# A gated delta rule kernel: triangular inverses from 16x16 blocks on all 128 partitions instead of 32x32 blocks on 64

## What is computed

```python
kb = k * beta[..., None]
a_mat = jnp.where(strict, jnp.einsum('bhncd,bhnsd->bhncs', kb, k) * decay, 0.0)
l_mat = a_mat + eye
t_mat = lax.linalg.triangular_solve(l_mat, jnp.broadcast_to(eye, l_mat.shape), left_side=True,
                                    lower=True, unit_diagonal=True)
u = jnp.einsum('bhncs,bhnsd->bhncd', t_mat, v * beta[..., None])
...
def step(state, inp):
    qd, qkc, uc, wc, kd, gl = inp
    v_new = uc - jnp.einsum('bhcd,bhde->bhce', wc, state)
    o = jnp.einsum('bhcd,bhde->bhce', qd, state) + jnp.einsum('bhcs,bhse->bhce', qkc, v_new)
    state = state * gl[..., None, None] + jnp.einsum('bhcd,bhce->bhde', kd, v_new)
    return state, o
```

## Time and profile before

| | |
|---|---|
| median of 3 runs | 2483.99 us (2482.22 to 2491.87) |
| profiled execution, its time | 2487.21 us |
| profiled execution, its span | 2485.4 us |
| PE busy in the span | 2140.9 us (86%) |
| DVE busy in the span | 1197.3 us (48%) |
| ACT busy in the span | 850.7 us (34%) |
| mean granted PE clock | 0.933 of 2.4 GHz |

### The profile page before, as it was taken

The page is one execution under the profiler, slowest core; times in us unless marked ns, Lnnn a source line. Parts: engine busy times, 40 slices in busy tenths (PEclk is TensorE's granted clock), DMA queues, the critical chain, the costliest instruction groups (busy, mean ns, idle before and its releaser), DMA issues. The chain is left out here.

```text
span 2485.4 us, 29399 instructions
## 1 busy us (share of the span) xinstructions
PE 2140.9 (86%) x11304; PEld 1677.7 (67%) x11304; DVE 1197.3 (48%) x2121; ACT 850.7 (34%) x1348; POOL 492.6 (20%) x280
## 2 busy tenths in 40 slices
PE   3589999999999999567984789999899886999978
PEld 2467878787787878545763577666676655788767
DVE  5658677585958577345223433324223232522243
ACT  2365253435345352134112132433433442510121
POOL 0220202021110202034354221111111101432240
PEclk7789999999999999778997899999999998999989
DMA  6123232222323231164112211120211105211222
GB/s 272 36 73 99 61 101 90 69 88 69 94 63 104 65 101 48 41 236 147 45 35 80 76 56 34 51 77 26 79 50 34 60 26 195 85 51 43 76 85 85
DMA packets 126523, 199.22 MB, mean 80 GB/s; under 512 B 56324, under 2 KB 87812, under 8 KB 125232
## 3 DMA queue, kind: packets, MB, share of 16 engines
q1 hardware_dynamic: 126384, 197.34, 24.6%
HBM read 155.17 MB, written 42.11 MB: 79 GB/s over the span
## 5 line engine op out<-in xcount | busy, mean ns | idle before, releaser
L709 PE MATMUL p_job<-h_hi,w_hi 128*128 128x512 f32 x784 | 332.0, 424 | 45.9 <-DVE w_lo L850 23.1
L711 PE MATMUL p_job<-h_hi,w_lo 128*128 128x512 f32 x784 | 312.6, 399 | 0.0
L710 PE MATMUL p_job<-h_lo,w_hi 128*128 128x512 f32 x784 | 312.4, 398 | 0.0
L1691 PE MATMUL m_job<-h_hi,m_hi 128*128 128x512 f32 x592 | 262.0, 442 | 36.8 <-POOL m_lo L1527 36.8
L1693 PE MATMUL m_job<-h_hi,m_lo 128*128 128x512 f32 x592 | 238.4, 403 | 0.0
L1692 PE MATMUL m_job<-h_lo,m_hi 128*128 128x512 f32 x592 | 237.7, 402 | 0.0
L709 PEld LDWEIGHTS p_job<-h_hi,w_hi 128*128 128x128 f32 x784 | 151.6, 193 | 88.7 <-DVE w_lo L850 23.4
L1527 POOL TENSOR_TENSOR m_lo<-m_raw,m_hi 128x1024 fp32r<-128x1024 f32 x37 | 89.9, 2429 | 465.4 <-DVE m_hi L1799 465.4
L710 PEld LDWEIGHTS p_job<-h_lo,w_hi 128*128 128x128 f32 x784 | 151.7, 194 | 37.5 <-issue 8.2
L711 PEld LDWEIGHTS p_job<-h_hi,w_lo 128*128 128x128 f32 x784 | 151.2, 193 | 33.0
L1691 PEld LDWEIGHTS m_job<-h_hi,m_hi 128*128 128x128 f32 x592 | 115.3, 195 | 83.0 <-POOL m_lo L1527 37.5
(11 more groups left out here) (350 smaller groups left out, 4592.4 us busy)
## 6 DMA issues: line engine op xcount, KB each, us to landing
w_raw<-in_w SPq DMA_DIRECT2D x49, 512.0 KB, 3.6
m_raw<-in_w SPq DMA_DIRECT2D x37, 512.0 KB, 3.6
rows<-grows SPq DMA_DIRECT2D x32, 512.0 KB, 6.5
ada<-in_ada_w SPq DMA_DIRECT2D x8, 1536.0 KB, 12.5
e_raw<-in_w SPq DMA_DIRECT2D x24, 512.0 KB, 3.6
z_scr<-pre SPq DMA_DIRECT2D x16, 512.0 KB
o_scr<-oT SPq DMA_DIRECT2D x64, 128.0 KB, 1.8
ob<-o_scr SPq DMA_DIRECT2D x16, 512.0 KB, 4.2
```

What stands on the lines that cost most here:

```text
L709: nc.tensor.matmul(p_job[h][:], hi, h_hi[:, k, cut], start=(k == 0), stop=False)
L710: nc.tensor.matmul(p_job[h][:], hi, h_lo[:, k, cut], start=False, stop=False)
L711: last = nc.tensor.matmul(p_job[h][:], lo, h_hi[:, k, cut], start=False, stop=(k == KD - 1))
L1691: nc.tensor.matmul(p_job[h][:], hi, h_hi[:, k, cut], start=(k == 0), stop=False)
```

## The change

Blocks of 16x16 (`SUB`) take the place of 32x32 ones in the substitution. There are two of them in each 32x32 block, 128 in all, one to each partition: partitions 0 to 63 hold the upper left halves, 64 to 127 the lower right ones. The substitution has 15 steps instead of 31, in three `lane` entries of five steps, on (j+1)x(15-j) elements. Two new merges on PE (now `merge` 0 and 1, the old four are 2 to 5) make the 32x32 inverses from the 16x16 ones:

```diff
-LANE_STEPS = 8
+SUB = 16
+LANE_STEPS = 3
+MERGES = 6
+MERGE_ACT = (0, 0, 4, 5, 7, 8)
+MERGE_DVE = (0, 1, 4, 5, 6, 7)
@@ plan
-            behind.append((15, ("silu", j)))
+            behind.append((10, ("silu", j)))
...
     for q in range(LANE_STEPS):
         out.append(("lane", q))
-        send(5)
-        if ahead and q == 2:
-            out.append(("bcast", i))
-    out.extend([("lanes_out",), ("diag_in",)])
-    send(80 - sent)
+        send(2)
+    out.append(("lanes_out",))
+    send(10)
+    if ahead:
+        out.append(("bcast", i))
+    out.append(("diag_in",))
+    send(72 - sent)
     if ahead:
         out.append(("decay", i, 0))
-    for q in range(4):
+    for q in range(MERGES):
         out.append(("merge", q))
         send(4)
@@ stage_deltanet, tiles
-        nsq = PM[:].rearrange("p u t -> p (u t)")[:, 0:HALF]
-        nrm = PM[:].rearrange("p u t -> p (u t)")[:, HALF:2 * HALF]
+        nsq = sb("nsq", [P, HALF])[:]
+        nrm = sb("nrm", [P, HALF])[:]
@@ SP
-                            sp.dma_start(AL[0:LANES], io["a_lanes"]).then_inc(al_in, 16)
+                            for q in range(2):
+                                sp.dma_start(AL[lane_rows(q)], halves(io["a_lanes"], q)).then_inc(al_in, 16)
...
-                            sp.dma_start(io["u_lanes"], UL[0:LANES]).then_inc(ul_out, 16)
+                            for q in range(2):
+                                sp.dma_start(halves(io["u_lanes"], q), UL[lane_rows(q)]).then_inc(ul_out, 16)
                             sp.wait_ge(turned, g + 1)
-                            sp.dma_start(io["t_lanes"], TL[0:LANES]).then_inc(ul_out, 16)
+                            for q in range(2):
+                                sp.dma_start(halves(io["t_lanes"], q), TL[lane_rows(q)]).then_inc(ul_out, 16)
@@ ACT, merge
+                            if q == 1:
+                                for n in range(NB):
+                                    nc.scalar.activation(Uu[blk(n), :, n * BLK + SUB:(n + 1) * BLK],
+                                                         grid(p_turn, n * BLK, (n + 1) * BLK, SUB, 0, 16), ACT.Copy
+                                                         ).then_inc(merge_act, 1)
@@ PE, merge
                                 for u in range(2 * NT):
+                                    for n in range(NB):
+                                        left = TD[blk(n), u, corner(n).start:corner(n).start + SUB]
+                                        last = nc.tensor.matmul(p_mone[blk(n), u * SUB:(u + 1) * SUB],
+                                                                atu[blk(n), u, blk(n)], left, start=True, stop=True)
+                            elif q == 1:
+                                pe.wait_ge(vb_done, 4 * (g + 1))
+                                for u in range(2 * NT):
+                                    for n in range(NB):
+                                        last = nc.tensor.matmul(
+                                            p_turn[blk(n), u * SUB:(u + 1) * SUB], PF[blk(n), u, :],
+                                            Uu[blk(n), u, n * BLK + SUB:(n + 1) * BLK], start=True, stop=True)
+                                for u in range(2 * NT):
+                                    for n in range(NB - 1):
+                                        last = nc.tensor.matmul(
+                                            p_mtwo[blk(n), u * SUB:(u + 1) * SUB], Uu[blk(n), u, blk(n)],
+                                            PF[blk(n), u, 0:SUB], start=True, stop=True)
@@ DVE, lane and merge
-                            for j in range(4 * q, min(4 * q + 4, BLK - 1)):
-                                m, r, w = N_LANE * g + 2 * j, j + 1, BLK - 1 - j
+                            for j in range(5 * q, 5 * q + 5):
+                                m, r, w = N_LANE * g + 2 * j, j + 1, SUB - 1 - j
...
+                                nc.vector.scalar_tensor_tensor(PF[:, :, 0:SUB], grid(p_mone, 0, P, SUB, 0, 16),
+                                                               fold[:, 2 * SUB:2 * SUB + 1],
+                                                               bc(fold[:, 0:SUB], 1, 2 * NT), ALU.mult, ALU.add
+                                                               ).then_inc(merge_dve, 1)
+                            elif q == 1:
+                                for n in range(NB - 1):
+                                    at_col = corner(n).start
+                                    nc.vector.tensor_copy(TD[blk(n), :, at_col:at_col + SUB],
+                                                          grid(p_mtwo, n * BLK, (n + 1) * BLK, SUB, 0, 16)
+                                                          ).then_inc(merge_dve, 1)
```

More of the change, by code:

```diff
@@ L432, in blk, with halves, lane_rows, corner @@
             return slice(n * BLK, (n + 1) * BLK)
+        def halves(scratch, q):
+            return scratch[:, q * SUB:(q + 1) * SUB, q * SUB:(q + 1) * SUB]
+        def lane_rows(q):
+            return slice(q * LANES, (q + 1) * LANES)
+        def corner(n):
+            return blk(1) if n == 1 else blk(0)
         def grid(bank, lo, hi, w, n0, n1):
@@ L447, in _ @@
                 for dst, src in ((tri[:], io["tri"]), (conv_w[:], io["conv_w"]),
-                                 (adt[32:48, :], io["adt"])):
+                                 (adt[32:48, :], io["adt"]), (fold[:], io["fold"])):
                     sp.dma_start(dst, src).then_inc(cst, 16)
+                sp.wait_ge(u_zero, 1)
+                for lanes in (io["u_lanes"], io["t_lanes"]):
+                    sp.dma_start(lanes.rearrange("u s t -> u (s t)"),
+                                 U[0:LANES].rearrange("p c a t -> p (c a t)")[:, 0:BLK * BLK]).then_inc(lanes_zero, 16)
                 load(1)
@@ L500, in _ @@
                                 sp.wait_ge(u_zero, 2)
-                            sp.wait_ge(ul_out, 32 * (g + 1))
-                            for n in range(NB - 1):
-                                cut = blk(1) if n == 1 else blk(0)
-                                sp.dma_start(TD[blk(n), :, cut], io["t_lanes"][n * 2 * NT:(n + 1) * 2 * NT].rearrange(
+                            sp.wait_ge(ul_out, 64 * (g + 1))
+                            for n in range(NB):
+                                sp.dma_start(TD[blk(n), :, corner(n)], io["t_lanes"][n * 2 * NT:(n + 1) * 2 * NT].rearrange(
                                     "u t s -> t u s")).then_inc(diag_in, 16)
@@ L626, in _ @@
                                 act.wait_ge(nss_done, m)
-                            if i >= 2 and w == 0 and h == 0:
-                                act.wait_ge(merge_ready, 4 * g)
                             nc.scalar.activation(nsq, src, ACT.Square).then_inc(nsq_done, 1)
@@ L674, in _ @@
                                                      ACT.Copy, scale=-1.0).then_inc(merge_act, 1)
-                            elif q == 2:
+                            elif q == 4:
                                 nc.scalar.activation(PM[64:128, 0:8, :], grid(p_mone, 64, 128, 2 * BLK, 0, 8),
                                                      ACT.Copy).then_inc(merge_act, 1)
-                            else:
+                            elif q == 5:
                                 nc.scalar.activation(Uu[0:64, 0:8, 64:128], grid(p_turn, 0, 64, 2 * BLK, 0, 8),
@@ L786, in _ @@
                                 for u in range(2 * NT):
+                                    for n in range(NB):
[5 more added lines that the diff above has]
+                                for u in range(2 * NT):
+                                    for n in range(NB):
+                                        last = nc.tensor.matmul(
[6 more added lines that the diff above has]
+                                            PF[blk(n), u, 0:SUB], start=True, stop=True)
+                            elif q == 2:
+                                for u in range(2 * NT):
                                     for r, bank in enumerate((p_mone, p_mtwo)):
@@ L987, in _ @@
                             if q == 0:
-                                dve.wait_ge(nmul, 4 * min(i + 1, QK_HEADS))
+                                if g >= 1:
+                                    dve.wait_ge(merge_dve, N_DVE * g)
+                                else:
+                                    dve.wait_ge(fold_set, 1)
+                                nc.vector.scalar_tensor_tensor(PF[:, :, 0:SUB], grid(p_mone, 0, P, SUB, 0, 16),
[8 more added lines that the diff above has]
+                                                          ).then_inc(merge_dve, 1)
+                            elif q == 2:
```

80 lines of the change are left out of this document (42 added, 38 removed).

## The result

The changed kernel takes 2500.57 us in the median (2497.46 to 2505.11), the kernel before 2484.68 us in the runs beside it (2482.22 to 2491.87). The ratio is 1.0061, with a 95% interval from 1.0034 to 1.0088. So it is slower by 0.6%, where 2461 us and a range from 2443 to 2492 us had been forecast.

What follows compares the result with a forecast made beforehand. PE was taken as the bound, busy 107 of 113 us per iteration. Terms -42.0 + 28.0 - 2.5 - 6.3 = -22.8 us gave 2464.4 from 2487.2, so 2461 us in the median; range 2443 to 2492, its own 2448 to 2472.

Steps and rivals of the forecast that it cites:

- New matmuls: New merges 0 and 1 on PE: 352 records cost 4.0 us per iteration, +28.0 us over seven iterations.
- PE's waits, -42.0: PE in iterations 1 to 7: evacuation and square waits go, 30.6 us, plus 11.4 us of lower clock.
- The square wait: PE waiting for ACT's squares, 1.60 us at 349.82, 12.1 us in iterations 1 to 7; read as the same ACT backlog.
- The four sub-arrays do not take turns: Rival at new merges: no overlap into one bank, 11.5 us per iteration, 2526 us; chance 0.16, in full 0.09.
- Half as many moving columns: Part of the bigger-gain rival (chance 0.13, about 2447 us): narrow matmuls in the new merges at half price, -12 us.
- The wait at the first sum: Rival: substitution in one run makes ACT's square late, PE waits 2 us or more per iteration; 2489 us, chance 0.17.
- Iteration 0, -2.5: Iteration 0: silus moved forward on ACT take 2.5 of the 5.4 us that PE waits for a square.
- Iteration 8, -6.3: Iteration 8: merging starts 14.7 us earlier, two more merges with copies in the open cost 8.4; net -6.3 us.
- Copies, DMAs, start: 0: New ACT and DVE copies under cover of slices, lane transfers, and constants at stage start: no cost, start bound +1.
- iteration of 110.4 us: Length of one iteration that the profile after the change was to show.

Runs made afterwards that it cites:

- the kernel with 11 matmuls left: Changed kernel with 11 small matmuls standing for the new merges' 176 from iteration 2 on, output not the reference's; 2448.29 us.
- the one with the halves apart by four and placed later: Changed kernel with four slices between merge 1's two halves, first merge at slice 70, decay step behind it, two slices between the last two merges; 2473.45 us.
- the swapped: Changed kernel with merge 1's two halves in the other order, the p_mtwo matmuls ahead of the p_turn ones; 2498.17 us.
- the extended kernel: Kernel before the change, with 112 extra small matmuls at the head of its merge 1, results used nowhere; 2545.48 us.

## Why the prediction was wrong

**The step that failed** is "New matmuls", +28.0 us. It priced 352 records by the time of the sub-arrays and the change-over, and asked nothing about how they reach PE. As work the price was right: merge 0 held PE for 1.3 us as forecast, and with the stalls gone an iteration is 110.5 us, 3.3 over the 107.2 of the kernel with 11 matmuls left, where I had 4.0 for all of them. What was missing is the stall, 15.9 - 1.8 = 14.1 us in iterations 1 to 7, and the lower clock behind it. The changed kernel and the one with the halves apart by four and placed later differ by 114.4 - 110.5 = 3.9 us per iteration, 27 us in seven: 2.0 us of stall, the rest slow slices. That is almost the whole miss of +13.5 against -14. The rows of the kernel before could have raised the question: its merge 1 has 96 records at 10.4 ns, but only 192 instructions in a row, less than a block of 256. The density was there, the length was not.

The Trainium skill (Runtime: NRT & Kernel Launch, "Instruction fetch mechanics") says that each engine's sequencer refills its instruction memory in 16 KiB blocks of 256 instructions, and that the cost of crossing a block is mostly hidden. The packets here have that size. That the cost is hidden holds for the slices and for the old merges; it does not hold for 448 or 640 instructions in a row that PE would do in 2 to 3 us, where it is 1.6 to 2.3 us for the 448 and 3.4 us an iteration for the 640.

**PE's waits, -42.0.** Right in size: 5.5 us per iteration measured with the small matmuls nearly left out, 6.0 forecast. Half of the reason was wrong. The square wait was not the substitution's backlog "further on", but ACT's order; I had given that part of the change no value in iterations 1 to 7, so that the size came out is in part luck.

**The rivals.** The four sub-arrays do not take turns: 128 records into one bank in 1.26 us, against 4 us in turns. Half as many moving columns did not halve the price either: one sub-array's 32 records took 1.2 us with 32 columns and take 1.26 us with 16. The rule of the Trainium skill (TensorEngine Tiling (Array Packing), "Gotcha 1: PSUM Pressure") that different row tiles cannot use one bank at once does not show in these runs, where each row group writes partitions of its own. The wait at the first sum did not come either, although the substitution with its copy ended at 314.1 and not at 309.7: it took 7.6 us for my 7.2, and began 4 us late (306.5), behind a split that DVE ended only then. The 2489 us of that rival was right for an iteration that loses some 4 of its 6 us, not one that keeps them, as the text has it. I had a rival that lost by a slow merge, with the wrong mechanism.

**Iteration 0, -2.5.** Measured +0.3 (175.1 against 174.8 us): the silu went, the decay exponential and two table loads stand ahead of the square.

**Iteration 8, -6.3.** Measured -2.0. Merging starts 13.2 us earlier after the reset (1011.71 - 985.22 = 26.5 against 39.7 us), where I had 14.7. The merges take 26.4 us from the first to the chunk loop:

```profile
1011.71 1.90 PE L819 MATMUL p_mone<-TD,at 32*32 32x16 f32 x128 [5.39 <-issue]
...
1015.30 1.72 PE L825 MATMUL p_turn<-U,PF 32*32 32x16 f32 x114 [0.64 <-issue]
...
1019.04 1.68 PE L830 MATMUL p_mtwo<-PF,U 32*32 32x16 f32 x83 [1.80 <-issue]
...
1022.45 0.26 PE L837 MATMUL p_mone<-TD,at 32*32 32x32 f32 x1 [1.73 <-ACT U L694]
...
1038.10 1.20 PE L871 MATMUL p_head<-Dl,U 128*128 128x128 f32 x4 [0.28 <-DVE Dl L1071]
```

Before, that stretch was 15.2 us (1011.14 to 1026.29), so it grew by 11.2 us, where I had 8.4. The 2.8 us and the 1.5 us that merging starts later than forecast are the 4.3 that are missing. Of the 2.8, the stall, which is here too, is 1.80; ACT's four copies in the open cost 1.73, of which the forecast had 1.1; the rest is not followed up.

**Copies, DMAs, start: 0.** Right in iterations 1 to 7, where no merge waits for a copy.

**The rest of the difference.** In the profiled executions the stage ends 11.8 us later (1064.8 against 1053.0 for its last store), and the stages behind it, whose code is the same, take 1438.5 us against 1432.4. In the profiles of the other kernels here that last part lies between 1428.6 and 1439.9 us, in no order that fits their edits, and a kernel's runs scatter by 2 to 14 us. The profiled execution after is the slowest of its four. What makes this scatter was not tried and stays open.

**Sums.** The forecast's "iteration of 110.4 us" is not what its own terms give: -42.0 + 28.0 over seven iterations is 2.0 us each, 110.7 us. The 110.5 us of the kernel without the stalls is close to both. Its own range of 2448 to 2472 does not follow from the bounds given for the terms either (-12 and -2.9 below, +2.1, +2.5 and +1 above: 2446 to 2467). Neither changes the outcome.

## What to carry to other kernels

Count instructions, not only engine time: on this chip a run of small matmuls on four sub-arrays takes 8 ns a record and two instructions each, and once a run holds a whole block of 256 PE stands until the next block has come, then runs at the lower clock (0.50 for 2.7 us in iteration 2). Put a few long matmuls between such runs, but look at what the other engines have ahead of the copies there, since moving a merge by four slices gave back half of what the slices between had won. When two waits look like one backlog, undo the parts of the change one at a time: here each had its own cause.

## What was not expected of the hardware

- PE goes on 2.2 to 2.8 us after a block fetch begins (all stalls of iterations 1 to 7 in the changed, the swapped and the extended kernel), although the fetch's own packet takes 0.9 to 1.4 us. Where the rest goes, and what starts a fetch, no view shows.
- "issue" in the profile's rows covers two things that look alike: the instruction stream (1.6 to 2.3 us, at a place that moves by 41 or 42 records from iteration to iteration, behind 129 to 219) and a wait for DVE's PF pass (1.22 us each time, always ahead of the same half). The rows of the other engine and the place tell them apart.
- Four row groups that write to one PSUM bank, each to its own partitions, overlap fully: 9.8 ns a record from the first start to the last end (1.26 us for 128), where two row groups into two banks had 16 ns.
